# Three layers on 256 tokens: a new order of work in the attentions, and token rows for the experts turned on VectorE

## The reference

```python
x = first_block(x, ...)     # attention of 8 heads + pooling, then a convolving FFN
x = even_layer(x, ...)      # 8 "fox" heads and 8 "swa" heads, then a SwiGLU FFN
x = odd_layer(x, ...)       # sparse attention of 16 heads, then 8 experts
return rms_norm_2(x, final_norm)

def apply_rope(t, cos, sin):                      # t1, t2: halves of a head's 64 values
    return concatenate([t1 * cos - t2 * sin, t2 * cos + t1 * sin], axis=-1)

def dsa_attention(q, k, v, iq, ik, iw):           # sparse attention
    score = einsum('bqh,bqhs->bqs', iw, relu(einsum('bqhd,bsd->bqhs', iq, ik)))
    idx = top_k(where(causal, score, -inf), 64)   # the 64 best keys of each query
    ...                                           # softmax over these keys alone

def moe_swiglu(h, ...):                           # two experts per token
    for e in range(8):
        out += combine[:, e:e+1] * swiglu(t, w_gate[e], w_up[e], w_down[e])
```

## Time and profile before

| | before |
|---|---|
| three runs | 1276.46, 1279.21, 1279.95 us |
| median | 1279.21 us |
| profiled execution: its own time | 1281.6 us |
| profiled execution: span | 1280.0 us |
| VectorE busy | 677.7 us (53%) |
| ScalarE busy | 270.5 us (21%) |
| GpSimd busy | 75.0 us (6%) |

### The profile page before, as it was taken

One profiled execution on the slowest core, in us unless ns is written; L12 is line 12 of the kernel. 1 busy time (PEld: TensorE's weight loads), 2 busy tenths in 40 slices (PEclk: granted clock), 3 DMA queues, 4 the chain that ended last, 5 costly groups with the idle time before them and its releaser, 6 DMA issues.

```text
span 1280.0 us, 26719 instructions
## 1 busy us (share of the span) xinstructions
PE 1244.6 (97%) x10684; PEld 945.9 (74%) x10684; DVE 677.7 (53%) x1696; ACT 270.5 (21%) x714; POOL 75.0 (6%) x133
## 2 busy tenths in 40 slices
PE   6999999999999999999999999989999999999997
PEld 4768889999999768799999997767654455445444
DVE  5355564888888636556677678894531011101104
ACT  4332304111121513630000013245300000000001
POOL 0100000000000000000000000100010000000020
PEclk9999999999999999999999999989999999999999
DMA  9999884677777682136777784893599999999990
GB/s 358 414 399 407 306 295 135 204 260 276 280 260 248 233 295 99 49 131 236 286 257 276 280 301 173 342 317 123 203 394 406 413 416 407 407 422 409 406 366 35
DMA packets 74181, 368.78 MB, mean 288 GB/s; under 512 B 8355, under 2 KB 8611, under 8 KB 49338
## 3 DMA queue, kind: packets, MB, share of 16 engines
q1 hardware_dynamic: 56594, 271.22, 56.3%
q0 software_dynamic: 17520, 96.64, 20.0%
HBM read 347.76 MB, written 20.06 MB: 287 GB/s over the span
## 4 chain that ended last, share of the span: by engine, by line
PE 92%; DVE 5%; DMA 1%; ACT 1%; SPq 1%; issue 1%; DVEq 0%
PE banks L948 21%; PE banks L692 16%; PE banks L1275 13%; PE banks L935 11%; PE banks L1324 9%; PE banks L1299 5%; PE banks L717 4%; PE banks L781 2%; PE banks L821 2%; PE banks L1015 2%; DMA ring<-stream 1%; PE banks L877 1%; PE banks L888 1%; PE banks L861 1%; DVE arena L1790 1%
## 5 line engine op out<-in xcount | busy, mean ns | idle before, releaser
L1718 DVE CUSTOM_DVE_ANT_0 side<-side 128x1024 f32<-128x1024 f32 x128 | 151.0, 1219 | 33.7 <-DMA side<-ada 33.6
L1275 PE MATMUL banks<-ring,arena 128*32 128x512 f32 x1536 | 166.3, 592 | 0.7 <-DVE arena L2204 0.7
L935 PE MATMUL banks<-arena,ring 128*128 128x256 f32 x704 | 158.6, 379 | 0.0
L692 PE MATMUL banks<-h,ring 128*128 128x256 f32 x640 | 143.9, 384 | 0.3
L935 PEld LDWEIGHTS banks<-arena,ring 128*128 128x128 f32 x704 | 130.7, 190 | 16.1
L692 PEld LDWEIGHTS banks<-h,ring 128*128 128x128 f32 x640 | 122.0, 192 | 20.5 <-issue 3.1
L1275 PEld LDWEIGHTS banks<-ring,arena 128*32 128x32 f32 x1536 | 50.0, 110 | 112.0 <-issue 110.9
L2307 DVE TENSOR_TENSOR arena<-arena,banks 128x256 f32<-128x256 f32 (+1 forms) x48 | 15.1, 328 | 178.4 <-ACT arena L1653 178.4
L692 PE MATMUL banks<-arena,ring 128*128 128x256 f32 x384 | 84.3, 380 | 0.5 <-ACT arena L1465 0.5
L948 PEld LDWEIGHTS banks<-h,ring 128*128 128x128 f32 x672 | 81.4, 192 | 2.2
L948 PE MATMUL banks<-arena 128*128 128x128 f32 x672 | 81.9, 275 | 0.0
(11 more groups left out here) (329 smaller groups left out, 1558.8 us busy)
## 6 DMA issues: line engine op xcount, KB each, us to landing
ring<-stream SPq DMA_DIRECT2D x247, 512.0 KB, 5.5
ring<-experts SPq DMA_DIRECT2D x96, 1024.0 KB, 15.1
side<-ada POOLq DMA_DIRECT2D x64, 1024.0 KB, 7.6
side<-experts SPq DMA_DIRECT2D x24, 1024.0 KB, 15.1
arena<-experts SPq DMA_DIRECT2D x8, 1024.0 KB
yrows<-side POOLq DMA_DIRECT2D x1, 6144.0 KB
hrows<-side POOLq DMA_DIRECT2D x1, 5632.0 KB
arena<-lasts SPq DMA_DIRECT2D x8, 512.0 KB
```

The source lines that it names most:

```text
L692: last = pe.matmul(bank(u, a, a + T), ring[:, s, (k0 + kc) * P:(k0 + kc + 1) * P], moving[:, kc, :], start=(kc == 0), stop=(kc == kn - 1))
L935: last = pe.matmul(banks[:, 4 + c // 2, (c % 2) * T:(c % 2 + 1) * T], ring[:, s, c * P:(c + 1) * P], hid[:, j % 2, :], start=first and c % ...
L1275: ins = pe.matmul(banks[BLOCK * j:BLOCK * (j + 1), t, :], hg[:, k, BLOCK * t:BLOCK * (t + 1)], ring[:, m, (j % 2) * 512:(j % 2 + 1) * 512] ...
L1718: dve.tensor_tensor_reduce(weights, weights, cond[:, 0 if layer0 else 1, :], 1.0, 0.0, ALU.mult, ALU.add, accum_out=msum[:, n:n + 1]).then ...
```

## The change

1. In the even and the sparse attention, TensorE's first-head transposes stand right behind the scores and ahead of the step's fillers. ScalarE takes the second head's exponentials behind the first head's transposed copy, and projections last. In all three attentions VectorE ends one head's softmax and then starts another's, in turns. Early output blocks go up to k = 6 (before: 4).
2. In the even layer the swa key is projected ahead of the queries, one filler in a step, and each swa pair waits only for its own rotation.
3. In the sparse attention ScalarE makes the shifted copies of the queries (four of 32 partitions) out of PSUM, and VectorE's rotation has three instructions. The key rotations go in 12 steps between the sums of the index scores. One small matmul (`rrow`) moves from the attention into the value projection, and ScalarE takes it.
4. For the experts, rows are written to HBM in an order such that four DMAs, each of 32 partitions with three pieces of 1 KB, load a pass into `hgrows`, and one 32x32 block transpose of VectorE over 128x768 makes `hg`. TensorE's row transposes and the copies behind them are gone.

```diff
-    add(("sq", 0), 1)
-    for c in range(1, 4):
+    add(("sk", 0), 1)
+    for c in range(4):
         add(("sq", c), 1)
-    add(("sk", 0), 1)
...
+            def rows_load(rows):
+                for m in range(QUADS):
+                    pool.dma_start(hgrows[BLOCK * m:BLOCK * (m + 1), :].rearrange("b (t n) -> b t n", t=BLOCKS),
+                                   rows[:, T * m:T * (m + 1)].rearrange("(t b) n -> b t n", t=BLOCKS)).then_inc(rows_in, 16)
...
-                pool.wait_ge(s_hgt, p)
-                pool.dma_start(hgtok[0:CAP, :], hrows[bass.ds((p + 1) * CAP, CAP), :]).then_inc(rows_in, 16)
+                pool.wait_ge(s_hg_low, p + 1)
+                rows_load(hrows[bass.ds((p + 1) * CAP, CAP), :])
...
+                    first = heads is first_heads
+                    if 1 <= m <= len(pairs) and not first:
+                        transposes(pairs[m - 1][0])
                     for step in between.get(2 * m, []) + between.get(2 * m + 1, []):
                         step()
-                    if 1 <= m <= len(pairs):
+                    if 1 <= m <= len(pairs) and first:
                         transposes(pairs[m - 1][0])
...
-                if not first:
-                    pe.wait_ge(s_hid, HIDS * p + BLOCKS)
-                    row_transposes(p)
...
+            def take_query(c):
+                u = U["dq", c]
+                act.wait_ge(*u.done)
+                act.wait_ge(s_rope, 10 + c)
+                for j in range(4):
+                    to, at = slice(BLOCK * j, BLOCK * (j + 1)), slice(BLOCK * (j ^ 1), BLOCK * (j ^ 1) + BLOCK)
+                    act.activation(ropet[to, c % 3, :], banks[at, u.bank, 0:T], ACT.Copy, scale=1.0 if j % 2 else -1.0).then_inc(s_shift, 1)
+                take(u, dqT[:, c, :], 0, T)
...
-                    if m < len(pairs):
-                        softmax_start(pairs[m][0])
-                        softmax_start(pairs[m][1])
-                    if m >= 1:
-                        softmax_end(pairs[m - 1][0])
-                        softmax_end(pairs[m - 1][1])
+                    for half in range(2):
+                        if m >= 1:
+                            softmax_end(pairs[m - 1][half])
+                        if m < len(pairs):
+                            softmax_start(pairs[m][half])
...
+            def query_rotation(c):
+                r, tile = 12 + c, dqT[:, c, :]
+                part = ropet[:, r % 3, :]
+                dve.wait_ge(s_shift, 4 * c + 4)
+                dve.tensor_tensor(part, part, sin[:, :], ALU.mult).then_inc(s_rot, 1)
+                dve.wait_ge(*taken(U["dq", c]))
+                dve.tensor_tensor(tile, tile, cos[:, :], ALU.mult).then_inc(s_rot, 1)
+                dve.wait_ge(s_rot, 60 + 2 * c + 2)
                 dve.tensor_tensor(tile, tile, part, ALU.add).then_inc(s_rope, 1)
...
+                if 1 <= m <= 6:
+                    head = (m - 1) // 3
+                    for step in range(2 * ((m - 1) % 3), 2 * ((m - 1) % 3) + 2):
+                        key_rotation(10 + head, dkT[:, head, :], ("dk", head), step)
...
+            def rows_turned(p):
+                dve.wait_ge(rows_in, 64 * (p + 1))
+                dve.transpose(hg.rearrange("p t c b -> p (t c b)"), hgrows).then_inc(s_hg_low, 1)
...
-                if not first:
-                    rows_in_place()
...
+                rows_turned(p)
```

More of the change, by code:

```diff
@@ L183, in plan_units @@
     add(("dk", 1), 1)
+    add("rrow")
     add("dv", 2)
-    add(("dq", 0), 1)
-    for c in range(1, 8):
+    for c in range(8):
         add(("dq", c), 1)
-        if c == 4:
-            add("rrow")
     add_out("oo")
@@ L883, in values @@
                 pe.wait_ge(s_pt, pair[1].n + 1)
+                if pair[0].kind == "swa" and pair[0].i == 0:
+                    pe.wait_ge(*taken(U["sv"]))
                 if done >= 1:
@@ L1155, in index_scores, with shift_row @@
                   .then_inc(s_iscore, 1)
+            def shift_row():
+                u = U["rrow"]
+                begin(u)
+                pe.wait_ge(s_raw, raw_step(4, 7))
+                pe.matmul(bank(u, 0, 8), ones[:, :], bwsum, start=True, stop=True).then_inc(aux_done, 1)
             index_scores(0)
@@ L1175, in _ @@
             pe.wait_ge(s_relu, 8)
-            between = {}
-            def shift_row():
-                u = U["rrow"]
-                begin(u)
-                pe.wait_ge(s_raw, raw_step(4, 7))
-                pe.matmul(bank(u, 0, 8), ones[:, :], bwsum, start=True, stop=True).then_inc(aux_done, 1)
-            for c in range(4, 9):
-                between[2 * (c - 4)] = between.get(2 * (c - 4), []) + [dq(c)] + ([shift_row] if c == 4 else [])
-            for k in range(5):
-                between[2 * (5 + k)] = between.get(2 * (5 + k), []) + [early_out("oo", dqT, 12, k)]
+            between = {2 * (c - 4): [dq(c)] for c in range(4, 8)}
+            for k in range(7):
+                m = max(4, 3 + k)
+                between[2 * m] = between.get(2 * m, []) + [early_out("oo", dqT, 12, k)]
             attend(odd_heads, between)
             pe.wait_ge(s_o, 20)
-            out_units("oo", 5, dqT, 5)
+            out_units("oo", 5, dqT, 7)
             def token_chunks(t):
@@ L1362, in _ @@
                 expert_pass(p)
-            pe.wait_ge(s_hg_low, passes + 1)
-            pe.wait_ge(s_hg_high, passes + 1)
             combine()
@@ L1453, in attend @@
                 for m in range(len(pairs) + 2):
+                    steps = between.get(2 * m, []) + between.get(2 * m + 1, [])
+                    first = heads is first_heads
                     if m < len(pairs):
                         exps(pairs[m][0])
-                        exps(pairs[m][1])
-                    for step in between.get(2 * m, []) + between.get(2 * m + 1, []):
-                        step()
+                        if first:
+                            exps(pairs[m][1])
+                    if first:
+                        for step in steps:
+                            step()
                     if 1 <= m <= len(pairs):
                         transposed(pairs[m - 1][0])
+                    if m < len(pairs) and not first:
+                        exps(pairs[m][1])
                     if m >= 2:
@@ L1467, in attend @@
                         transposed(pairs[m - 1][1])
+                    if not first:
+                        for step in steps:
+                            step()
             def ffn(name, conv):
```

124 lines of the change are left out of this document (60 added, 64 removed).

## The result

| | before | after |
|---|---|---|
| runs, median | 1278.84 us (4 runs, 1276.46 to 1279.95) | 1264.80 us (4 runs, 1263.85 to 1267.53) |
| ratio | | 0.9891, 95% interval 0.9872 to 0.9909 |
| profiled execution, own time | 1281.6 us | 1263.85 us |
| its span | 1280.0 us | 1262.2 us |
| mean granted clock in it | 0.992 | 0.999 |

The change is 14.0 us faster (11.6 to 16.4 by the interval); 11.6 were forecast. Run again later beside other runs of the kernel before, the changed kernel was 11.0 us faster (ratio 0.9914, 7.8 to 14.2). The two profiled executions differ by 17.8, more than either; why is told in the first experiment.

A forecast was written before the change was run, and what follows sets the result against it. TensorE, busy 97% of the span, was taken as the bound. Passes −5.3, sparse attention −4.9 and even layer −1.4 sum to −11.6 us; against the median of 1279.21 that gave 1267.6 us, with bounds 1262.8 to 1272.3.

The forecast's parts named there:

- Passes, −5.3: Expert passes: row transposes leave TensorE, −5.7 us, and +0.4 ahead of the loop; bounds −5.7 and −2.7.
- The junction's term: Between the pass ahead of the loop and the loop: VectorE's turn of 0.94 replaces a copy of 0.55, +0.4 us.
- 7 x 0.81: Seven loop passes over the experts: each loses 0.81 us of TensorE's row transposes, −5.7 us.
- it still fits: Expert weight loads: landing grows 1.5 us a pass to 24 us, within the 35.8 at which a ring slot is wanted.
- Sparse attention, −4.9: Sparse attention: −8.0 us of waits and slow work removed, +3.1 of new waits; bounds −8.0 and −3.8.
- (a): Sparse attention: first softmax at 834.6, so the first transposes wait 0.6 us; bounds 0 and 1.7.
- (b): Sparse attention: first early output block waits 1.15 us for ScalarE's last query shifts and take; bounds 0 and 1.15.
- (c): Sparse attention: twice, back-to-back transposes wait 0.67 us for ScalarE's copy, 1.34 us in all; bounds 0 and 1.34.
- Even layer, −1.4: Even layer's attention: waits of 2.0 and 0.67 us removed, 1.34 new; projections change places free; bounds −2.7 and −0.4.
- keep the pass: Rival, expert passes: full DMA queues hold each at 43.60 us, so passes give +0.4; 1273.3 us, chance 0.10.
- the second rival: Both attentions: waits move to ScalarE and VectorE, 0.5 us more for each of 16 pairs, +8.0; 1275.6 us, chance 0.12.
- the slower one: Rival, both attentions: transposes wait for VectorE's softmax end in all 16 steps, 1.4 us each; 1285.6 us, chance 0.07.

The follow-up runs named there:

- the first experiment: The kernel before, run again unchanged with a profile of its own: median 1279.19 us of ten runs, ratio 1.001 to before.

## Why the prediction was right

**Passes, −5.3.** Measured −6.65 in D and +0.24 at the junction: −6.4. The mechanism was right. The junction's term was +0.4; the term 7 x 0.81 was mis-sized, since a pass loses 0.95 (306.67 − 300.02, over 7). The down product is 0.14 shorter directly behind the up product; what in it is shorter was not looked into.

**Queues.** The step that said "it still fits" was right in its outcome and about right in its limit (36.3 us where 35.8 was said), but the growth was mis-sized: 2.3 us a pass where 1.5 was forecast, 26.8 us in the sixth pass of the loop where 24 was the end of the sum. The shorter pass is in the sum; the lower rate is not. The rate is 411 GB/s before, 404 after, 386 with the rows loaded twice. That fits the rule of the Trainium skill (Perfetto Trace Analysis, DMA Optimizations) that small DMAs under 2 KB have overhead, but does not show it: four loads stand in place of one, and no run loads the rows twice in large pieces. The reading of the earlier trace rows, that rows of three 1 KB pieces count as packets of 3 KB, was wrong: by the trace's packet sizes there is none of 3 KB. The results' store, in such rows, is 64 packets of 2 KB and 64 of 4 KB in a pass, and so is the new load.

**Sparse attention, −4.9.** Measured −5.25. The waits that went are those that the sum named. Of the new waits, (a) was 0.6 and is none: the first softmax comes at 830.0, which is 834.0 on the old time against 834.6, and the transposes follow it sooner than the 3.5 us taken from the old rows. (b) was 1.15 and is 1.30. (c) was two waits of 0.67 and is two waits of 0.67. The first rotation's wait for ScalarE was 2.2 and is 2.63. ScalarE was late for VectorE in three more rotations, which the prediction had named as a sign of being wrong; it cost nothing, as TensorE was not waiting for these. The reason given, that VectorE is early, is only part of it: by the profiles the order and ScalarE's shifts each lose on their own, and the prediction did not see that they need each other.

On the price of a shift, rows decided: four copies took 1.57 us on ScalarE, 0.39 each, against 0.38 assumed. The estimate of 0.51 us from the Trainium skill (ScalarE: Activation LUTs, Rules for kernel authors) did not apply: the budget there is for an ACTIVATE whose bias is a `[128,1]` operand, and these copies have none (arena<-banks in their rows). The same rules send plain multiplies to VectorE; here VectorE took 0.44 us for a shift, 0.05 more than ScalarE, and with the shifts on VectorE the stage was 6.1 us longer.

**Even layer, −1.4.** Measured −0.9 in stage A, by the profile only. Both terms were right in size (2.65 us of waits gone, 1.34 new); of the 0.4 between, 0.1 is a new wait ahead of the output projection, and the rest lies in TensorE's busy time and was not looked into. But the cause was not the one given. With the old order the old waits are gone all the same, one of 0.67 us stands in their place, and A is 297.18; so the new order brought the 1.34 and not the gain, and the gain came from the dealing of the projections, which the prediction priced at nothing ("only change places"), or from VectorE's turns. That the sum came near is luck.

**Sum.** −11.6 forecast; −12.6 by stages; −14.0 and, run again, −11.0 by the medians, with intervals that hold both. The passes gave 1.1 more than forecast and the even layer 0.5 less, so the errors partly cancel.

**Rivals.** The queues did not keep the pass, though 384 KB more in each pass made them its bound. No transposes wait for VectorE's softmax end, and for ScalarE's copy only the four of 0.67 us that the sum had, so neither the second rival nor the slower one took place. The conditions of the slower one exist when ScalarE does not shift: a wait of 2.52 us, once.

## What to carry to other kernels

Cost an edit by the stage it stands in, and compare stages between markers: here most repeat within 0.2 us at the same clock, while the runs of one kernel spread over 5. Compare an execution that has a stretch at the low clock with one that has the same stretch. Take the parts of a change out alone and in pairs: by the profiles, the order alone or the shifts alone cost 4.5 and 6.1 us of the stage, both together 2.5; and a wait may be gone for another reason than the one in the sum. And ask how full a hidden queue is before calling it hidden: doubling the rows' load told more than the sum of its bytes. Count a load's lateness from the release of its slot, not from its issue, since the issue can be late itself.

## What was not expected of the hardware

The granted clock behind the same idle time of 0.91 us, in stages that no edit touched, was 0.83 on the mean of ten microseconds in some executions (part of them at 1.2 in place of 2.4 GHz) and 1.00 in others, at 1.3 to 1.7 us a time; the runs of the kernel before lie from 1275.8 to 1281.6 us, with a mean clock of 0.992 or 0.993 in those over 1281 us and 0.995 to 0.998 in those under 1277. A second load of the rows, in pieces of 1 KB, lowered the rate of the full queues from 404 to 386 GB/s; whether the pieces do this or any further load would was not tested. And with the queues that far behind, SyncE's issues took up to 8.7 us in place of 0.33.
